# Eight of the 22 row tiles of a down projection taken by block products of half size

## The chip, the cores and the metric

One core of a Trainium2 chip runs the whole program. The metric is the device time of one execution in microseconds (us). The engines are named as in the profile: PE (matmuls), DVE (vector), ACT (scalar), POOL, and SP, which issues the weight transfers.

## What is computed

Five blocks of a transformer in a row, on 512 tokens of width 1024, all in fp32. Each block is a mixer (state space and banded attention in the first; stick-breaking, differential attention or a short convolution, and an attention over a memory, in the four of the second part) and then a gated feed-forward part, which is what the change touches:

```python
D_FF = -(-8 * D_MODEL // (3 * 256)) * 256        # 2816 = 22 tiles of 128
x = x + (jax.nn.silu(h2 @ w_gate[l]) * (h2 @ w_up[l])) @ w_down[l]

def _swiglu(x, w_in, w_out):
    gu = x @ w_in
    return (jax.nn.silu(gu[..., :D_FF_2]) * gu[..., D_FF_2:]) @ w_out
```

The five feed-forward parts have the same sizes: 1024 to 2 x 2816 and 2816 to 1024.

## The kernel before

Tensors lie with the feature on the partitions: `x` is 8 tiles of 128 features x 512 tokens. To keep fp32 accuracy every operand is split into a high part (rounded, made by ACT) and a low part (the rest, made by DVE as raw minus high), and every product is three matmuls: high x high, high x low, low x high. The code calls the parts `hh, hl`, `acth, actl`, `whi, wlo`, `wh, wl`.

Weights stream in *units*: 128 partitions x 2048 elements in one of two slots of `raw`. SP loads a unit when the low part of the unit before it is made (`lo_made`), ACT makes its high part when the unit that held the slot is used up (`unit_used`; `ahead`, `high`), DVE its low part (`low`), and PE waits for that (`unit_ready`). All engines run their own fixed program in order and meet at counting semaphores, so an instruction that waits holds up everything behind it on its engine.

A feed-forward part (`swiglu(s, u0, gc, r)` on each engine) has 34 units, u0 to u0+33. Units u0 and u0+1 are taken with plain matmuls. The next 20 units (10 turns of two, gate and up columns) go through `seven`: the 8 row tiles and the 2 column tiles of a unit are a 2 x 2 block matrix, and seven block products replace eight. A product is 4 row tiles x 3 matmuls of 256 tokens, 12 matmuls, and a unit has 84. PE's order in a unit is A11, S1, A22 *of the unit before*, S2, A12, S4, S3. For that DVE makes sums of weight blocks (`first_sums`, `sum_s2`, `sum_s4`), the low parts of all seven forms (`corner_low`, `sum_low`, `odd_low`, `sums_low`), a correction in PSUM of the unit before (`take_late`, counted by `late_made`, for which A22 waits), and the result of the unit before (`finish`): the gate goes to `gs`, and the product with the up half to `actr`, 22 tiles of unscaled activations. Turns 1 to 8 are a hardware loop; turns 0 and 9 are written out.

The down projection is two column halves of 512, each six units (five of 4 row tiles, one of 2), with 4 column tiles in 4 PSUM banks: 48 matmuls of 512 tokens in a full unit, 24 in the short one. `scale_tiles` multiplies `actr` by the row factor of the norm and a sign just before the high part of these tiles (`act_high`) and their low part (`act_low`, `tile_lows`) are made; `down_lows` puts scaling, `low` and `act_low` in a row for each unit. During the first unit of the down stage, PE does the last A22 product, and DVE finishes the last pair of tiles (20, 21).

## Time and profile before

| | |
|---|---|
| median of 3 runs | 3000.03 us (2999.93 to 3000.07) |
| the profiled execution | 3000.31 us, of which the span is 2998.6 us |
| granted clock of PE over the span | 0.999 |
| PE busy | 2982.5 us, 99% |
| DVE busy | 2086.0 us, 70% |
| ACT busy | 1384.7 us, 46% |
| DMA | 283.18 MB, mean 94 GB/s |

The span is what the profile shows of an execution; 1.7 us lie around it. Matmuls are pipelined, and the duration that a row shows for one (0.28 us at 256 tokens, 0.39 us at 512) is longer than the distance to the next one's start. A short wait of PE hides in that overlap and is not counted as idle, so the time of PE has to be read from starts, not from its busy time.

### The profile page before, as it was taken

The numbers are of one execution on the slowest core, as the hardware profiler recorded it, in microseconds if no ns is written. First come the engines' busy times: TensorE is split into PE (matmuls) and PEld (weight loads), VectorE is DVE, ScalarE is ACT, GpSimd is POOL, SyncE is SP. The second block draws the span as 40 slices with busy tenths as digits, with TensorE's granted clock in tenths as the row PEclk, the third lists the DMA queues.
The fourth block names the chain that finished last, engine by engine and source line by source line (L and its number), as shares of the span: only waits on it lengthen the run. The fifth ranks groups of instructions, "written<-read, shape, count | busy, mean of one in ns | idle before, by whom it ended". The sixth has DMA issues, their size and how long they took to land.

```text
span 2998.6 us, 46083 instructions
## 1 busy us (share of the span) xinstructions
PE 2982.5 (99%) x18093; PEld 2636.0 (88%) x18093; DVE 2086.0 (70%) x2497; ACT 1384.7 (46%) x1969; POOL 58.7 (2%) x148
## 2 busy tenths in 40 slices
PE   9999999999999999999999999999999999999998
PEld 8779998888889998878899988789998878899987
DVE  7978886466759884466598854658886457588862
ACT  3576553354445553334455533325554244365533
POOL 6100000000000000000000000000000000000000
PEclk9999999999999999999999999999999999999999
DMA  6122332342133233211333323223232222232322
GB/s 188 49 75 88 108 117 93 110 135 71 55 100 99 98 112 98 85 59 59 106 101 98 112 92 102 88 67 116 98 107 97 92 85 65 63 112 98 112 92 77
DMA packets 246445, 283.18 MB, mean 94 GB/s; under 512 B 11874, under 2 KB 208672, under 8 KB 246312
## 3 DMA queue, kind: packets, MB, share of 16 engines
q1 hardware_dynamic: 246200, 281.28, 29.2%
q8 instruction: 97, 1.59, 0.2%
q14 instruction: 36, 0.29, 0.0%
q10 hardware_dynamic: 112, 0.02, 0.0%
HBM read 279.16 MB, written 4.73 MB: 95 GB/s over the span
## 4 chain that ended last, share of the span: by engine, by line
PE 95%; DVE 3%; ACT 1%; issue 1%; DMA 0%; POOL 0%; ACTq 0%; POOLq 0%; SPq 0%; DVEq 0%
PE ps L2689 33%; PE ps L2318 17%; PE ps L2320 17%; PE ps L2319 17%; PE ps L2985 1%; PE ps L2986 1%; PE ps L2987 1%; PE ps L2892 1%; PE ps L2952 1%; PE ps L2931 1%; PE ps L2971 1%; PE ps L2972 1%; PE ps L2973 1%; PE ps L2821 1%; PE ps L2841 1%
## 5 line engine op out<-in xcount | busy, mean ns | idle before, releaser
L1390 DVE TENSOR_TENSOR wlo<-raw,whi 128x2048 fp32r<-128x2048 f32 (+2 forms) x169 | 350.8, 2076 | 415.6 <-ACT whi L787 415.3
L787 ACT ACTIVATE whi<-raw 128x2048 fp32r<-128x2048 f32 (+2 forms) x169 | 294.6, 1743 | 746.9 <-PE ps L2320 693.0
L2689 PE MATMUL ps<-th,wh 128*128 128x256 f32 x1600 | 453.7, 284 | 0.6 <-DVE wl L1475 0.5
L2689 PE MATMUL ps<-tl,wh 128*128 128x256 f32 x1600 | 452.7, 283 | 0.0
L2689 PE MATMUL ps<-th,wl 128*128 128x256 f32 x1600 | 452.7, 283 | 0.0
L2318 PE MATMUL ps<-hh,whi 128*128 128x512 f32 x896 | 357.3, 399 | 1.0 <-DVE uf L1857 1.0
L2320 PE MATMUL ps<-hh,wlo 128*128 128x512 f32 x896 | 349.7, 390 | 0.0
L2319 PE MATMUL ps<-hl,whi 128*128 128x512 f32 x896 | 349.3, 390 | 0.0
L2318 PE MATMUL ps<-acth,whi 128*128 128x512 f32 x880 | 342.7, 389 | 0.0
L2319 PE MATMUL ps<-actl,whi 128*128 128x512 f32 x880 | 342.5, 389 | 0.0
L2320 PE MATMUL ps<-acth,wlo 128*128 128x512 f32 x880 | 342.4, 389 | 0.0
L2689 PE MATMUL ps<-hh,wh 128*128 128x256 f32 x1200 | 340.0, 283 | 0.1
L2689 PE MATMUL ps<-hh,wl 128*128 128x256 f32 x1200 | 339.6, 283 | 0.0
L2689 PE MATMUL ps<-hl,wh 128*128 128x256 f32 x1200 | 339.6, 283 | 0.0
L2689 PEld LDWEIGHTS ps<-th,wh 128*128 128x128 f32 x1600 | 307.0, 192 | 2.3 <-DVE wl L1475 1.1
L2689 PEld LDWEIGHTS ps<-tl,wh 128*128 128x128 f32 x1600 | 307.0, 192 | 0.2
L2689 PEld LDWEIGHTS ps<-th,wl 128*128 128x128 f32 x1600 | 307.1, 192 | 0.0
L2689 PEld LDWEIGHTS ps<-hh,wh 128*128 128x128 f32 x1200 | 230.3, 192 | 0.8 <-DVE gs L1526 0.3
L2689 PEld LDWEIGHTS ps<-hl,wh 128*128 128x128 f32 x1200 | 230.4, 192 | 0.2
L2689 PEld LDWEIGHTS ps<-hh,wl 128*128 128x128 f32 x1200 | 230.3, 192 | 0.0
L2318 PEld LDWEIGHTS ps<-hh,whi 128*128 128x128 f32 x896 | 168.4, 188 | 38.8 <-issue 6.1
L2320 PEld LDWEIGHTS ps<-hh,wlo 128*128 128x128 f32 x896 | 168.2, 188 | 36.0
(472 smaller groups left out, 5706.5 us busy)
## 6 DMA issues: line engine op xcount, KB each, us to landing
raw<-in_w_ffn_in SPq DMA_DIRECT2D x88, 1024.0 KB, 5.1
raw<-in_w_in SPq DMA_DIRECT2D x59, 1024.0 KB, 5.3
raw<-in_w_ffn_out SPq DMA_DIRECT2D x40, 1024.0 KB, 5.0
raw<-in_w_o SPq DMA_DIRECT2D x32, 640.0 KB, 4.3
raw<-in_w_gate SPq DMA_DIRECT2D x11, 1024.0 KB, 5.3
raw<-in_w_up SPq DMA_DIRECT2D x11, 1024.0 KB, 5.4
raw<-in_w_down SPq DMA_DIRECT2D x10, 1024.0 KB, 5.0
raw<-in_w_mem_kv SPq DMA_DIRECT2D x8, 1024.0 KB, 5.4
```

What stands on the lines that cost most here:

```text
L787: a.activation(whi[:, slot, 0:n], raw[:, slot, 0:n], ACT.Copy).then_inc(hi_made, 1)
L1390: v.tensor_tensor(wlo[:, u % 2, 0:n], raw[:, u % 2, 0:n], whi[:, u % 2, 0:n].bitcast(F32), ALU.subtract).then_inc(lo_made, 1)
L2318: mm(dst, wh, xh, start=first, stop=False, skip_group_check=True)
L2319: mm(dst, wh, xl, start=False, stop=False, skip_group_check=True)
L2320: return mm(dst, wl, xh, start=False, stop=last, skip_group_check=True)
L2689: e = mm(bank(b, HALF), wgt[:, q, w], xx, start=start and k == 0 and m == 0, stop=k == KD // 2 - 1 and m == 2, skip_group_check=True)
L2821: e = mm(bank(b + r, MEM, MEM * i), mq[rows, f, t:t + P], km[rows, l, f, :], start=i == 0, stop=True, skip_group_check=True)
L2841: e = mm(ps[64 * r:64 * r + 64, o:o + 256], vm[:, l, j, MD * h:MD * h + MD], mt[:, j, 256 * r:256 * r + 256], start=j == 0, stop=j == 1, s ...
L2892: e = tr(ps[:, o:o + P], stick[:, ZQ[i] + P * j:ZQ[i] + P * j + P], ident[:, :])
L2931: e = mm(bank(6 + d, T - P * j, P * j), vp[hd % 2][:, j, P * d:P * d + P], dpt[:, ZK[j]:ZK[j] + wk(j)], start=j == 0, stop=j == 3, skip_gr ...
L2952: e = mm(ps[:, ZQ[i]:ZQ[i] + wq(i)], qp[hd % 2][:, c, P * i:P * i + P], kp[hd % 2][:, c, 0:wq(i)], start=i != 2, stop=True, skip_group_che ...
L2971: mm(dst, hs, whi[:, slot, w], start=k == 0, stop=False, skip_group_check=True)
```

## The change

In each of the five down projections the row tiles 8 to 15 are taken out of the two column halves. They are multiplied for all 1024 columns in four units of 8 row tiles x 256 columns, with seven half-size products each, like the units of the up loop. The order of units is now: column half 0 with row tiles 0 to 3, 4 to 7, 20 and 21, 16 to 19 (units u0+22 to u0+25); the four new units (u0+26 to u0+29); column half 1 with row tiles 0 to 3, 4 to 7, 16 to 19, 20 and 21 (u0+30 to u0+33). The number of units and of bytes is the same.

The result of a new unit is added to two tiles of `x` by DVE (`run_added`), column half 0 is added to `x` in `half_in`, and column half 1 as before. The new units need the activations in blocks: four sums of blocks of 4 tiles x 256 tokens (`run_t`), their high and low parts (`run_th`, `run_tl`), and the parts of the even and odd tiles (`even_hi`, `odd_hi`); `down_run` is DVE's program for this. Scaling leaves the down stage: turn i of the up loop, from 1 to 9, ends with the scaling of its pair of tiles; pair 10 is scaled at the start of `down_run`.

Two edits lie elsewhere: the first eviction of the first projection is cut in two, so that PE waits only for one tile, and the small operations `lambda_and_distance` of the differential attention come three slots earlier.

```diff
-                pair_loop(2, u0 + 22, 4, 512, lambda j: (wd, 4 * j, min(4, KF - 4 * j), 0, 512), per=6)
+                for d in range(12):
+                    u = u0 + 22 + d
+                    if 4 <= d < 8:
+                        load(u % 2, KD, 256, wd[:, 8:16, 256 * (d - 4):256 * (d - 4) + 256], u - 1)
+                    else:
+                        t, c0 = down_rows(d), 512 * (d >= 8)
+                        n = min(4, KF - t)
+                        load(u % 2, n, 512, wd[:, t:t + n, c0:c0 + 512], u - 1)
...
+                if j and not (isinstance(i, int) and i == 0):
+                    dve.wait_ge(acc_free, at_turn(i, 2, gc + 2))
+                    v.tensor_tensor(tiles_of_pair(i), tiles_of_pair(i), rs2[:, :, :], ALU.mult).then_inc(act_scaled, 1)
...
+            def run_added(s, u0, n):
+
+                dve.wait_ge(unit_used, u0 + 27 + n)
+                dve.wait_ge(late_made, LATES * s + 21 + n)
+                ab, bb, _ = RUN[n % 2]
+                first = v.tensor_tensor(x[:, 2 * n, :], x[:, 2 * n, :], bank(ab), ALU.add)
+                second = v.tensor_tensor(x[:, 2 * n + 1, :], x[:, 2 * n + 1, :], bank(bb), ALU.subtract)
+                if n < 2:
+                    first.then_inc(x_new, 1)
+                    second.then_inc(x_new, 1)
+                else:
+                    second.then_inc(acc_free, 1)
...
+            def down_run(s, u0, gc):
+
+                p, first = u0 % 2, u0 + 26
+                dve.wait_ge(acc_free, gc + 22)
+                v.tensor_tensor(tiles_of_pair(10), tiles_of_pair(10), rs2[:, :, :], ALU.mult).then_inc(act_scaled, 1)
+                dve.wait_ge(act_scaled, SCALED * s + 7)
+                dve.wait_ge(product_done, PRODUCTS * s + 120)
+                v.tensor_tensor(run_t[0][:, :, :], run_half(0, 0), run_half(0, 1), ALU.subtract).then_inc(sum_made, 1)
+                v.tensor_tensor(run_t[2][:, :, :], run_half(1, 1), run_half(0, 1), ALU.subtract).then_inc(sum_made, 1)
+                dve.wait_ge(sum_made, SUMS * s + 65)
+                v.scalar_tensor_tensor(out=run_t[1][:, :, :], in0=run_half(1, 1), scalar=-1.0, in1=run_t[0][:, :, :],
+                                       op0=ALU.mult, op1=ALU.subtract).then_inc(sum_made, 1)
+                dve.wait_ge(sum_made, SUMS * s + 67)
+                v.scalar_tensor_tensor(out=run_t[3][:, :, :], in0=run_t[1][:, :, :], scalar=-1.0, in1=run_half(1, 0),
+                                       op0=ALU.mult, op1=ALU.subtract).then_inc(sum_made, 1)
+                dve.wait_ge(ffn_hi, FFN_HIS * s + 20)
+                tile_lows(20, 2)
+                for k, t in enumerate((0, 2)):
+                    moved_low(s, t, 21 + k)
+                dve.wait_ge(ffn_hi, FFN_HIS * s + 23)
+                tile_lows(16, 4)
+                low(u0 + 24)
+                dve.wait_ge(sum_made, SUMS * s + 68)
+                for k, t in enumerate((1, 3)):
+                    moved_low(s, t, 24 + k)
+                dve.wait_ge(ffn_hi, FFN_HIS * s + 26)
+                v.tensor_tensor(actl[:, 8:16:2, 0:HALF], run_half(0, 0), even_hi[:, :, :].bitcast(F32), ALU.subtract).then_inc(ffn_lo, 1)
+                dve.wait_ge(ffn_hi, FFN_HIS * s + 27)
+                v.tensor_tensor(actl[:, 9:16:2, :], actr[:, 9:16:2, :], odd_hi[:, :, :].bitcast(F32), ALU.subtract).then_inc(ffn_lo, 1)
+                low(u0 + 25)
+                dve.wait_ge(loaded[p], 16 * (first // 2 + 1))
+                first_sums(p, True)
+                corner_low("A11", p, p, form_hi, FORM_HIS * s + 101, form_lo)
+                corner_low("A12", p, p, form_hi, FORM_HIS * s + 102, form_lo)
+                dve.wait_ge(sum_made, SUMS * s + 69)
+                sum_s2(p, p, True)
+                sum_low("S1", p, form_hi, FORM_HIS * s + 103, form_lo, True)
+                dve.wait_ge(sum_made, SUMS * s + 70)
+                sum_s4(p, p, True)
+                sum_low("S2", p, form_hi, FORM_HIS * s + 104, form_lo, True)
+                half_in(s, u0, gc, range(3))
+                sum_low("S4", p, form_hi, FORM_HIS * s + 105, form_lo, True)
+                corner_low("A22", p, p, form_hi, FORM_HIS * s + 106, lo_made)
+                for n in range(4):
+                    run_step(s, u0, gc, n)
+                dve.wait_ge(ffn_hi, FFN_HIS * s + 28)
+                low_half(u0 + 30, 0, ffn_lo)
+                run_late(s, 3)
+                dve.wait_ge(hi_made, plain_units(u0 + 30) + 1)
+                low_half(u0 + 30, 1, lo_made)
+                run_added(s, u0, 3)
+                low(u0 + 31)
...
                 tile_lows(0, 1)
-                scale_tiles(2, 2)
...
                 tile_lows(2, 2)
-                down_lows(s, u0, (1,))
+                low(u0 + 23)
+                dve.wait_ge(ffn_hi, FFN_HIS * s + 19)
+                tile_lows(4, 4)
                 dve.wait_ge(unit_used, u0 + 22)
...
                 finish(s, STREAMED, 1)
+                down_run(s, u0, gc)
...
-            down_lows(0, U_GU1, range(2, 8))
...
-                        v.tensor_tensor(phases, src.rearrange("p (a c s) -> p a c s", a=2, s=4), row, ALU.mult).then_inc(acc_free, 1)
+                        src = src.rearrange("p (a c s) -> p a c s", a=2, s=4)
+                        if u == 0:
+                            v.tensor_tensor(phases[:, 0:1], src[:, 0:1], row[:, 0:1], ALU.mult).then_inc(S("first_tile"), 1)
+                            phases, src, row = phases[:, 1:2], src[:, 1:2], row[:, 1:2]
+                        v.tensor_tensor(phases, src, row, ALU.mult).then_inc(acc_free, 1)
...
-                if s == DZ[0] - 2:
+                if s == DZ[0] - 5:
...
+            def run_unit(s, u0, gc, r, n):
+
+                p, (ab, bb, db) = u0 % 2, RUN[n % 2]
+                even = lambda k: (even_hi[:, k, :], actl[:, 8 + 2 * k, 0:HALF])
+                odd = lambda h: lambda k: (odd_hi[:, k, HALF * h:HALF * h + HALF], actl[:, 9 + 2 * k, HALF * h:HALF * h + HALF])
+                t_ = lambda m: lambda k: (run_th[m - 1][:, k, :], run_tl[m - 1][:, k, :])
+                form = lambda k: pe.wait_ge(form_lo, FORM_LOS * s + (80 + (1, 3, 2, 4, 5)[k] if n == 0 else 81 + 4 * n + (2, 3, 4, 4, 4)[k]))
+                snap = lambda k: pe.wait_ge(snap_taken, SNAPS * s + 60 + 3 * n + k)
+                form(0)
+                if n == 0:
+                    pe.wait_ge(acc_free, gc + 22)
+                    pe.wait_ge(ffn_lo, FFN_LOS * s + 19)
+                elif n == 1:
+                    pe.wait_ge(acc_free, gc + 23)
+                else:
+                    pe.wait_ge(x_new, KD * (r + 1) + 2 * n - 2)
+                product("A11", p, even, ab, start=True).then_inc(product_done, 1)
+                form(1)
+                product("S1", p, t_(1), db, start=True).then_inc(product_done, 1)
+                if n:
+                    run_corner(s, u0, n - 1)
+                form(3)
+                snap(1)
+                product("S2", p, t_(2), bb).then_inc(product_done, 1)
+                if n == 0:
+                    form(2)
+                else:
+                    pe.wait_ge(lo_made, u0 + 27 + n)
+                product("A12", p, odd(0), ab).then_inc(product_done, 1)
+                form(4)
+                snap(2)
+                product("S4", p, odd(1), db).then_inc(product_done, 1)
+                pe.wait_ge(form_lo, FORM_LOS * s + 86 + 4 * n)
+                snap(3)
+                product("S3", p, t_(3), bb).then_inc(product_done, 1)
...
+                    if d == 0:
+                        pe.wait_ge(acc_free, gc + 21)
+                    elif d < 4:
+                        unit_ready(u0 + 22 + d)
+                        pe.wait_ge(ffn_lo, FFN_LOS * s + (11, 12, 15)[d - 1])
+                    elif d == 8:
+                        pe.wait_ge(ffn_lo, FFN_LOS * s + 20)
+                        pe.wait_ge(acc_free, gc + 24)
+                    else:
+                        unit_ready(u0 + 22 + d)
...
+                for d in range(4):
+                    down(d)
+                for n in range(4):
+                    run_unit(s, u0, gc, r, n)
+                for d in range(8, 12):
+                    down(d)
```

The first place is the end of the loop of turns on DVE. Before, the last instructions of turn 8's second unit are the result to `gs` (L1526), the low parts of two corners (L1469) and of two sums (L1475); then the loop branches, a scaling of tiles 0 and 1 stands once behind the loop (L1642), and the correction for which A22 waits is L1516:

```order
L1469 TENSOR_TENSOR wl_57<-raw,wh_55 128x2x512
L1473 REGISTER_ALU
L1475 TENSOR_TENSOR wl_57<-stmp,wh_55 128x2x512
L1639 REGISTER_ALU
L1639 COMPARE_AND_BRANCH
L1642 TENSOR_TENSOR actr<-actr,rs_63 128x1024
L1516 TENSOR_TENSOR ps<-ps,us 128x2x256
```

In the changed kernel, where L1556, L1562 and L1603 are the same three operations:

```order
L1556 TENSOR_TENSOR wl_57<-raw,wh_55 128x2x512
L1560 REGISTER_ALU
L1562 TENSOR_TENSOR wl_57<-stmp,wh_55 128x2x512
L1653 REGISTER_ALU
L1654 TENSOR_TENSOR actr<-actr,rs_63 128x1024
L1826 REGISTER_ALU
L1826 COMPARE_AND_BRANCH
L1829 TENSOR_TENSOR actr<-actr,rs_63 128x1024
L1603 TENSOR_TENSOR ps<-ps,us 128x2x256
```

One scaling has come in ahead of the loop's branch, so it stands between L1562 and the L1603 of the next turn in every turn of the loop; behind the loop there are two in a row.

The second place is DVE in the first units of the down stage. Before, from the product of the last pair (L1524) on, with scalings (L1587), low parts of weight units (L1390) and of activations (L1573):

```order
L1524 TENSOR_TENSOR actr<-ps,gs 128x1024
L1587 TENSOR_TENSOR actr<-actr,rs_63 128x2048
L1390 TENSOR_TENSOR wlo<-raw,whi 128x2048
L1573 TENSOR_TENSOR actl<-actr,acth 128x2048
L1587 TENSOR_TENSOR actr<-actr,rs_63 128x2048
L1390 TENSOR_TENSOR wlo<-raw,whi 128x2048
```

In the changed kernel, up to the low part of weight unit u0+24 (L1476), for which PE's unit d = 2 waits. L1611 is the product of the last pair, L1723 its scaling, L1726 to L1732 are the block sums, L1775 and L1778 low parts of activations:

```order
L1611 TENSOR_TENSOR actr<-ps,gs 128x1024
L1723 TENSOR_TENSOR actr<-actr,rs_63 128x1024
L1726 TENSOR_TENSOR run_t_151<-actr 128x1024
L1727 TENSOR_TENSOR run_t_153<-actr 128x1024
L1729 SCALAR_TENSOR_TENSOR run_t_152<-actr,run_t_151 128x1024
L1732 SCALAR_TENSOR_TENSOR run_t_154<-run_t_152,actr 128x1024
L1778 TENSOR_TENSOR actl<-actr,acth 128x1024
L1775 TENSOR_TENSOR run_tl_159<-run_t_151,run_th_155 128x1024
L1775 TENSOR_TENSOR run_tl_161<-run_t_153,run_th_157 128x1024
L1778 TENSOR_TENSOR actl<-actr,acth 128x2048
L1476 TENSOR_TENSOR wlo<-raw,whi 128x1024
```

and from there to the low part of weight unit u0+25, which PE's unit d = 3 waits for:

```order
L1775 TENSOR_TENSOR run_tl_160<-run_t_152,run_th_156 128x1024
L1775 TENSOR_TENSOR run_tl_162<-run_t_154,run_th_158 128x1024
L1745 TENSOR_TENSOR actl<-actr,even_hi 128x4x256
L1747 TENSOR_TENSOR actl<-actr,odd_hi 128x4x512
L1476 TENSOR_TENSOR wlo<-raw,whi 128x2048
```

Between the product of the last pair and the next weight unit's low part there stood one scaling of 2048 elements; now there stand nine instructions there, and four between that low part and the following unit's, where two stood.

## Rows read from the trace of the kernel before

**Rows 1.** The page, part 1: engine, busy us (share of span) xinstructions.
```profile
PE 2982.5 (99%) x18093; PEld 2636.0 (88%) x18093; DVE 2086.0 (70%) x2497; ACT 1384.7 (46%) x1969; POOL 58.7 (2%) x148
```

**Rows 2.** Who the matmuls waited for, whole span: us, times, longest.
```profile
PE ps L2318 <- DVE uf L1857: 1.0, 1, 1.0
PE ps L2916 <- DVE lam L2111: 0.5, 1, 0.5
```

**Rows 3.** Timeline of ACT, up loop: start us, us, instruction, idle before.
```profile
383.06 0.37 ACT L880 ACTIVATE ps<-ps 128x256 f32<-128x256 f32 x1 [0.73 <-PE ps L2689]
...
390.34 1.06 ACT L859 ACTIVATE wh<-stmp 128x1024 fp32r<-128x1024 f32 x1 [0.31 <-PE ps L2689]
...
393.14 0.37 ACT L880 ACTIVATE ps<-ps 128x256 f32<-128x256 f32 x1 [0.81 <-PE ps L2689]
```

**Rows 4.** Timeline of ACT, down stage, two weight units in sequence.
```profile
474.92 1.92 ACT L787 ACTIVATE whi<-raw 128x2048 fp32r<-128x2048 f32 x1 [3.51 <-PE ps L2320]
...
485.80 1.92 ACT L787 ACTIVATE whi<-raw 128x2048 fp32r<-128x2048 f32 x1 [7.16 <-PE ps L2320]
```

**Rows 5.** Windows: one turn of the up loop, and most of the down stage.
```profile
320.84:341.00 20.16, 20.16 (x171) 20.16 (x170) 16.83 (x20) 11.06 (x17) 0.00 (x0) 1.00 0.33 104
474.64:530.00 55.36, 55.36 (x246) 45.83 (x245) 28.14 (x16) 20.77 (x16) 0.00 (x0) 1.00 0.29 94
```

**Rows 6.** Timeline of DVE, a steady boundary of two turns.
```profile
381.35 1.23 DVE L1475 TENSOR_TENSOR wl<-stmp,wh 128x1024 fp32r<-128x1024 f32 x1 [0.22 <-ACT wh L859]
382.49 0.69 DVE L1516 TENSOR_TENSOR ps<-ps,us 128x512 f32<-128x512 f32 x1
...
390.06 1.23 DVE L1469 TENSOR_TENSOR wl<-raw,wh 128x1024 fp32r<-128x1024 f32 x1 [1.48 <-ACT wh L856]
```

**Rows 7.** Timeline of PE: first matmuls of A22 and of S3.
```profile
384.30 0.28 PE L2689 MATMUL ps<-th,wh 128*128 128x256 f32 x1
...
390.06 0.28 PE L2689 MATMUL ps<-th,wh 128*128 128x256 f32 x1
```

**Rows 8.** Timeline of DVE, the boundary ahead of the last turn.
```profile
442.98 1.22 DVE L1642 TENSOR_TENSOR actr<-actr,rs 128x1024 f32<-128x1024 f32 x1
444.11 0.69 DVE L1516 TENSOR_TENSOR ps<-ps,us 128x512 f32<-128x512 f32 x1
```

**Rows 9.** Timeline of PE at that boundary, first and fifth swiglu.
```profile
444.66 0.28 PE L2689 MATMUL ps<-th,wl 128*128 128x256 f32 x1
444.95 0.35 PE L2689 MATMUL ps<-th,wh 128*128 128x256 f32 x1
445.14 0.28 PE L2689 MATMUL ps<-tl,wh 128*128 128x256 f32 x1
...
2845.92 0.28 PE L2689 MATMUL ps<-th,wl 128*128 128x256 f32 x1
2846.21 0.35 PE L2689 MATMUL ps<-th,wh 128*128 128x256 f32 x1
```

**Rows 10.** Source view of L1642: durations min/median/max ns, first and last start.
```profile
L1642 DVE TENSOR_TENSOR actr<-actr,rs x5: 1218/1218/1219, 443.0 to 2844.2; 128x1024 f32<-128x1024 f32 x5
```

**Rows 11.** Timeline of DVE, start of the down stage.
```profile
468.69 2.29 DVE L1390 TENSOR_TENSOR wlo<-raw,whi 128x2048 fp32r<-128x2048 f32 x1 [0.43 <-ACT whi L787]
470.90 2.28 DVE L1573 TENSOR_TENSOR actl<-actr,acth 128x2048 fp32r<-128x2048 f32 x1
473.10 1.22 DVE L1524 TENSOR_TENSOR actr<-ps,gs 128x1024 f32<-128x1024 f32 x1
474.24 2.28 DVE L1587 TENSOR_TENSOR actr<-actr,rs 128x2048 f32<-128x2048 f32 x1
```

**Rows 12.** Timeline of DVE, two scalar_tensor_tensor, the second needs the first.
```profile
248.78 1.22 DVE L1608 SCALAR_TENSOR_TENSOR traw<-hg,traw 128x1024 f32<-128x1024 f32 x1
250.03 1.22 DVE L1610 SCALAR_TENSOR_TENSOR traw<-traw,hg 128x1024 f32<-128x1024 f32 x1
```

**Rows 13.** Timeline of DVE: the eviction that L1857 is.
```profile
33.74 2.00 DVE L1857 TENSOR_TENSOR uf<-ps,rs 128x1024 f32<-128x1024 f32 x1
```

More of the change, by code:

```diff
@@ L369, in g_in @@
         def g_in(l):
-            return G_L0 + sum(evictions(m) + 22 for m in range(l))
+            return G_L0 + sum(evictions(m) + 25 for m in range(l))
         def g_gu(l):
@@ new lines, in sum_high, with moving_high, run_step @@
+            def sum_high(form, p, sem, run=False):
+                a.activation(wh8[:, place_of(form, p), :], temp_sum(run, form, p), ACT.Copy).then_inc(sem, 1)
+            def moving_high(s, t):
+                act.wait_ge(sum_made, SUMS * s + 65 + (0, 2, 1, 3)[t])
+                a.activation(run_th[t][:, :, :], run_t[t][:, :, :], ACT.Copy).then_inc(ffn_hi, 1)
+            def run_step(s, u0, n):
+                p, (ab, bb, db) = u0 % 2, RUN[n % 2]
+                slot = (u0 + n) % 2
+                done = lambda k: act.wait_ge(product_done, PRODUCTS * s + 120 + 6 * n + k)
+                summed = lambda k: act.wait_ge(sum_made, SUMS * s + 68 + 3 * n + k)
+                done(0)
+                summed(1)
+                sum_high("S3", p, form_hi, True)
+                done(1)
+                a.activation(bank(bb, HALF), bank(ab, HALF), ACT.Copy).then_inc(snap_taken, 1)
+                if n < 3:
+                    act.wait_ge(loaded[1 - slot], 16 * ((u0 + 27 + n) // 2 + 1))
+                    corner_high("A11", p, 1 - slot, form_hi)
+                done(2)
+                act.wait_ge(late_made, LATES * s + 20 + n)
+                a.activation(us[:, 1, 0:HALF], bank(db, HALF), ACT.Copy).then_inc(snap_taken, 1)
+                if n < 3:
+                    summed(4)
+                    sum_high("S1", p, form_hi, True)
+                done(3)
+                a.activation(us[:, 0, 0:HALF], bank(bb, HALF), ACT.Copy).then_inc(snap_taken, 1)
+                done(4)
+                if n == 3:
+                    high_half(u0 + 30, 0, ffn_hi)
+                    high_half(u0 + 30, 1, hi_made)
+                    return
+                act.wait_ge(unit_used, u0 + 26 + n)
+                odd_high(p, 1 - slot, 1 - n % 2)
+                done(5)
+                summed(6)
+                sums_high(p, True)
@@ new lines, in swiglu @@
+                moving_high(s, 0)
+                moving_high(s, 2)
+                act.wait_ge(unit_used, u0 + 22)
+                act_high(s, 16, 4, 9)
+                ahead(u0 + 22)
+                moving_high(s, 1)
+                moving_high(s, 3)
+                a.activation(even_hi[:, :, :], run_half(0, 0), ACT.Copy).then_inc(ffn_hi, 1)
+                a.activation(odd_hi[:, :, :], actr[:, 9:16:2, :], ACT.Copy).then_inc(ffn_hi, 1)
+                ahead(u0 + 23)
+                first = u0 + 26
@@ L975, in swiglu @@
+                sum_high("S4", p, form_hi, True)
+                corner_high("A22", p, p, form_hi)
+                for n in range(4):
+                    run_step(s, u0, n)
+                for d in range(7, 12):
+                    if d >= 8:
+                        ahead(u0 + 22, 0, 0, d)
+                    if d == 7:
+                        ahead(u0 + 29)
                         if between:
@@ L977, in swiglu @@
                         residual(r + 1, range(4))
+                    if d == 11:
+                        residual(r + 1, range(4, 7))
+                    if between and d in (9, 10):
+                        memory_high(range(4) if d == 9 else range(4, KD))
+                    if s == NL and d == 10:
+                        first_columns()
                 residual(r + 1, range(7, 8))
@@ L1395, in lows, with residual @@
                     low(u)
-            def residual(r, wait, src, mode, before={}, after={}, flush=(), amid={}):
+            def residual(r, wait, src, mode, before={}, after={}, flush=(), amid={}, given=0):
                 def finish(t):
```

350 lines of the change are left out of this document (195 added, 155 removed).

## The prediction

> **What bounds the kernel now.** I read the page's first part, then the list of waits of PE, then starts in the timeline. PE is busy 99% of the span and DVE 70% [rows 1]; the waits that the matmuls show are 1.0 us and 0.5 us at two single places, beside some smaller ones [rows 2]. So the time is the sum of PE's distances from start to start, and a change pays by fewer or shorter distances and costs by every wait that it puts on PE.
>
> Two distances price the change. In the up loop ACT copies the result of the first product of each unit (L880), once a unit: 383.06 and 393.14, so 84 matmuls of 256 tokens take 10.08 us, 0.120 us each [rows 3]. In the down stage ACT makes the high part of a weight unit when PE has left the unit before it: 474.92 and 485.80, so 48 matmuls of 512 tokens take 10.88 us, 0.2267 us each [rows 4]. ACT starts 0.28 us after PE is through: S3 starts on PE at 390.06, when S4 has ended, and ACT's L859, which waits for S4, at 390.34 [rows 3, 7]. So in the first feed-forward part PE leaves unit u0+22 at 474.92 - 0.28 = 474.64.
>
> **What is saved on PE.** 8 row tiles x 8 column tiles x 3 = 192 matmuls of 512 tokens are four full units, 43.52 us; the new ones are 4 x 10.08 = 40.32 us. Saved: 3.20 us for each of five parts, **16.0 us**. Transfers stay equal in number and bytes, and nothing in the down stage waits for them.
>
> The 256-token matmul here costs more than half of the 512-token one: half would be 0.1133 us, the row says 0.120 [rows 3, 4]. The Trainium skill ("TensorE: Matmul & The Clock Gate", Back-to-back issue gap) gives N / 2.4 + 2.5 ns for an isolated matmul at full clock, 109 ns and 216 ns. By its formula the saving would be 20 x (48 x 0.216 - 84 x 0.109) = 24 us, 8 us more. The row comes from the same form of product and decides.
>
> **What the scaling costs in the loop.** Per turn DVE is busy 16.83 of 20.16 us [rows 5], so 1.14 us more fits by the sum. But it is put where DVE is late. S4 of a unit ends on PE at 390.06 - 10.08 = 379.98; behind it come ACT's high part, DVE's low part of two sums (381.35), then the correction L1516, 382.49 to 383.18 [rows 6]. A22 waits for this correction and starts at 384.30 [rows 7]: 1.12 us of slack. The scaling is put between the two and takes 1.14 us. What that gives, the trace already shows, because L1642 is the same instruction in the same place, once in each part [rows 10]: it starts at 442.98, the correction moves to 444.11 to 444.80 [rows 8], PE starts A22 at 444.95 where 444.66 + 0.12 = 444.78 was due, and the next matmul follows after 0.19 instead of 0.12: 0.24 us lost, and the same 0.29 us distance stands in the fifth part [rows 9]. PE goes on 0.15 us after DVE's end.
>
> New scalings stand at the ends of turns 1 to 9. Those of turns 1 to 7 cost 0.24 us each, 1.68. That of turn 8 meets L1642, which stays behind the loop: two in a row, 1.14 us more in full. That of turn 9 is behind the last result, where DVE then waits for ACT's half unit anyway, and I cost it at nothing. Sum 2.82 us, times five **+14.1 us**. DVE does not fall behind further on, since it waits 1.48 us ahead of L1469 in the same turn [rows 6].
>
> **What DVE costs in the first down units.** DVE used to be idle nearly half of this stage: 28.14 of 55.36 us busy [rows 5]. The work for the new units comes in a burst. Lengths from start to start: 1.14 us for 1024 elements (473.10 to 474.24), 2.21 for 2048 (468.69 to 470.90) [rows 11], 1.25 for 1024 if the instruction needs the one before it (248.78 to 250.03) [rows 12]. The last pair's product starts at 473.10 as before, since nothing ahead of it on the path changes. From there, by the order shown: scaling of pair 10 at 474.35; four block sums at 475.49, 476.63, 477.77 and 479.02; low parts of tiles 20 and 21 at 480.16; of two sums at 481.30 and 482.44; of tiles 16 to 19 at 483.58; of weight unit u0+24 at 485.79, ended at 485.79 + 1.23 = 487.02. ACT, which takes 1.06 us for 1024 elements and 1.92 for 2048 [rows 3, 4], has the four copies after its copy of pair 10 and the unit's own high part done about 6 us after 475.5, ahead of DVE. PE needs the unit at 474.64 + 10.88 = 485.52 and gets it at 487.17: it waits **1.65 us**. It then has only the short unit, 24 matmuls, 5.44 us, to 492.61. DVE goes on: two low parts of sums at 486.93 and 488.07, even tiles at 489.21, odd tiles (2048) at 490.35, weight unit u0+25 at 492.56, ended at 494.85. PE gets it at 495.00 and waits **2.39 us** more. Sum 4.04 us, times five **+20.2 us**. I take the four other parts as equal, because the same instructions run there.
>
> The order of units makes this worse: the short unit, which gives DVE half the time, comes third, with the greatest backlog.
>
> **The new units themselves** I cost at nothing beyond their matmuls. Two additions of 512 elements take the place of the result of 1024, DVE's load per unit is that of a loop unit without scaling, and the first one has 3 us of room: DVE waits for PE to leave unit u0+25 for its last two low parts, S4 and A22, about 1.5 us after that, and S4 starts 4 x 1.44 = 5.8 us after. The going over to column half 1 is built like the one to column half 0, where PE's list of waits names nothing. Without that cover a unit would wait as the loop's boundary does, 0.24 us, 20 times: 5 us at most.
>
> **The two small edits.** The eviction that PE waits for 1.0 us [rows 2] takes 2.00 us [rows 13]; one tile of it takes half, so PE starts about 1 us sooner: -1.0, but this can be lost again in the attention that follows, where PE also waits for DVE. The lambda operations: -0.5 [rows 2], at least nothing. I take -1.5 together, with 0 as the other bound.
>
> **Sum.** 3000.31 of the profiled execution (span 2998.6 and 1.7 around it) - 16.0 + 14.1 + 20.2 - 1.5 = 3017.1; the median before is 0.3 below that execution, so 3016.8, rounded to **3017 us**, 0.57% slower.
>
> **Rivals.**
> *All hidden* (faster): PE's queue of loaded matmuls absorbs both waits, and only the saving is left, 3000.0 - 16.0 - 1.5 = 2982.5. For it: DVE has 30% idle over the span. Against it: L1642's wait is seen in every part, and the chain of DVE is a plain sum. Chance 0.08. It decides if DVE's burst were shorter by 4 us, for instance if the sums ran before the last pair's product.
> *Only one of the two waits is real* (no change): loop alone 2996.6, burst alone 3002.7. Chance 0.08.
> *The block products run at half the 512-token distance*, 0.1133 us: the saving is 20 x (10.88 - 9.52) = 27.2, and the time 3005.6. Nothing in the up loop speaks for it. Chance 0.02. The skill's formula above would be this side of the forecast, at 3009.
> *The new units wait too* (slower still): the chain of S4's and A22's forms, which starts only when u0+25 is used, or ACT, which has five copies there, makes PE wait 1 to 3 us per part: 3022 to 3032. Chance 0.12.
> *The clock falls* in the new waits: the granted clock is 1.00, so 2.4 GHz, in every window I read [rows 5], but none holds a wait of PE as long as 2.4 us. At 1.2 GHz a short unit of 5.44 us would cost 5.44 more, 27 us over five parts: 3044. Chance 0.02.
>
> **How the numbers follow.** The forecast, both waits real, has 0.68, with a range of its own of 3009 to 3022: the loop term between 0.17 and 0.30 us per turn (+-2.5), the burst between 3.2 and 4.6 us per part (+-4), the small edits 0 to 1.5. The whole range goes down over the half-distance case and up into the fourth rival: 3002 to 3026, which takes in the burst alone. A difference of 0.2%, 6 us, is what a measurement of this kernel tells from no change. Faster 0.08; within 0.2% (2994 to 3006) 0.10; slower 0.82.
>
> **What would show it.** In the changed trace: PE starts at A22 0.29 us after the matmul before it in turns 2 to 8 of each part, and some 1.4 us in turn 9; L1603 as the releaser. Waits of PE for L1476 of about 1.7 and 2.4 us at the third and fourth down unit, DVE without a gap from L1611 to the second of these. Units of 10.08 us and no waits between u0+26 and u0+29. The prediction is wrong if DVE shows gaps in that burst, if PE waits in the new units, or if no A22 is late in the loop.

## The result, and the profile after

The changed kernel takes 3019.11 us in the median of 5 runs (3018.17 to 3023.17), where the kernel before takes 3000.03 us in 5 runs beside it (2999.11 to 3000.45). The ratio is 1.0067, with a 95% interval of 1.0056 to 1.0079: slower by 19 us. The profiled execution took 3019.11 us, with a span of 3017.4 us. The forecast of 3017 us held.

Part 1 of the page answers to [rows 1], and the list of PE's waits over the span (us, times, longest) to [rows 2]:

```profile
PE 2979.5 (99%) x18813; PEld 2660.8 (88%) x18813; DVE 2254.2 (75%) x2773; ACT 1459.1 (48%) x2144; POOL 58.0 (2%) x148
```

```profile
PE ps L2509 <- DVE wlo L1476: 18.1, 13, 2.1
PE ps L2884 <- DVE ps L1603: 5.7, 5, 1.1
```

PE's busy time has gone down by 3 us and the span has gone up by 19, so the time lies in waits. DVE grew from 70% to 75% of the span, far from full. Both waits of [rows 2] are gone (L1857 and the lambda), and two new ones head the list. The wait for L1603 comes once in each of the five parts. That for L1476 comes twice in each (17.0 us together); the three other times are short ones, 0.35 us each, at the start of a layer (experiment 7).

**The loop.** PE at the correction's boundary, in a steady turn of part 1, in turn 9, and in a steady turn of part 2 (starts; the answer to [rows 9]):

```profile
303.01 0.28 PE L2884 MATMUL ps<-th,wl 128*128 128x256 f32 x1
303.30 0.36 PE L2884 MATMUL ps<-th,wh 128*128 128x256 f32 x1
303.49 0.28 PE L2884 MATMUL ps<-tl,wh 128*128 128x256 f32 x1
...
445.81 0.28 PE L2884 MATMUL ps<-th,wl 128*128 128x256 f32 x1
447.23 0.36 PE L2884 MATMUL ps<-th,wh 128*128 128x256 f32 x1 [1.15 <-DVE ps L1603]
...
953.48 0.28 PE L2884 MATMUL ps<-th,wl 128*128 128x256 f32 x1
953.67 0.39 PE L2884 MATMUL ps<-th,wh 128*128 128x256 f32 x1
953.90 0.28 PE L2884 MATMUL ps<-tl,wh 128*128 128x256 f32 x1
```

Two distances of 0.12 us are 0.24. At 303.01 they take 0.48: 0.24 us are lost, with no idle time shown, as forecast; for that reason the profile names no releaser in these turns. In part 2, and in the same way in parts 3 to 5, they take 0.42, so 0.18 is lost. In turn 9 the first distance alone is 1.42: 1.30 us lost, and 0.07 more at the next. DVE shows why: the scaling stands between the low part that A22's turn needs and the correction (compare [rows 6], where L1516 came 1.14 us behind L1475; here L1603 comes 2.28 behind L1562).

```profile
320.58 1.23 DVE L1562 TENSOR_TENSOR wl<-stmp,wh 128x1024 fp32r<-128x1024 f32 x1 [0.22 <-ACT wh L885]
321.72 1.22 DVE L1654 TENSOR_TENSOR actr<-actr,rs 128x1024 f32 x1
322.86 0.69 DVE L1603 TENSOR_TENSOR ps<-ps,us 128x512 f32<-128x512 f32 x1
```

**The burst.** DVE in the first down units, from the product of the last pair on (the answer to [rows 11]), and PE where it waits:

```profile
475.37 1.22 DVE L1611 TENSOR_TENSOR actr<-ps,gs 128x1024 f32<-128x1024 f32 x1
476.62 1.23 DVE L1723 TENSOR_TENSOR actr<-actr,rs 128x1024 f32<-128x1024 f32 x1
477.76 1.22 DVE L1726 TENSOR_TENSOR run_t<-actr 128x1024 f32<-128x1024 f32 x1
478.90 1.22 DVE L1727 TENSOR_TENSOR run_t<-actr 128x1024 f32<-128x1024 f32 x1
...
481.29 1.22 DVE L1732 SCALAR_TENSOR_TENSOR run_t<-run_t,actr 128x1024 f32<-128x1024 f32 x1
...
488.04 1.22 DVE L1476 TENSOR_TENSOR wlo<-raw,whi 128x1024 fp32r<-128x1024 f32 x1
...
494.78 2.28 DVE L1476 TENSOR_TENSOR wlo<-raw,whi 128x2048 fp32r<-128x2048 f32 x1
```

```profile
487.59 0.39 PE L2511 MATMUL ps<-acth,wlo 128*128 128x512 f32 x1
489.31 0.50 PE L2509 MATMUL ps<-acth,whi 128*128 128x512 f32 x1 [1.33 <-DVE wlo L1476]
489.65 0.39 PE L2510 MATMUL ps<-actl,whi 128*128 128x512 f32 x1
...
494.66 0.39 PE L2511 MATMUL ps<-acth,wlo 128*128 128x512 f32 x1
497.12 0.50 PE L2509 MATMUL ps<-acth,whi 128*128 128x512 f32 x1 [2.07 <-DVE wlo L1476]
```

DVE has no gap from 475.37 to the second weight unit. The matmul at 489.31 was due at 487.59 + 0.23 = 487.82: 1.49 us of wait. The one at 497.12 was due at 494.89: 2.23 us. The next matmul follows 0.34 us behind instead of 0.227, another 0.1 us each time. The idle figures in brackets (1.33, 2.07) are smaller than the waits, since the row's duration of 0.39 covers part of them.

The Trainium skill ("Perfetto Trace Analysis", Optimizing Scalar/DVE Operations) puts some 60 ns of data access on a DVE operation in SBUF and says that a profiled latency is longer than that, because the end of one operation overlaps the next; from that and the Trainium skill's 0.96 GHz for DVE ("VectorE: DVE Perf Modes", Specifications) an estimate for an operation of 1024 elements is 1.13 us. The rows agree: they last 1.22 us and follow each other after 1.14.

**The new units.** ACT's copy of the first product, once a unit, in units u0+27 and u0+28 (the answer to [rows 3]):

```profile
518.40 0.37 ACT L905 ACTIVATE ps<-ps 128x256 f32<-128x256 f32 x1 [0.81 <-PE ps L2884]
...
528.49 0.37 ACT L905 ACTIVATE ps<-ps 128x256 f32<-128x256 f32 x1 [0.81 <-PE ps L2884]
```

10.09 us, and the list shows no wait of PE in these units. Read from starts, the 336 matmuls of the four units follow each other after 0.120 us in the mean in every part, and none after more than 0.14 but one: there the first twelve matmuls of column half 1 stand ahead of the last A22 product.

**What the forecast did not have.** In part 2 the matmuls behind the second wait run at twice their distance (PE, starts), and the windows around it (length; PE, PEld, DVE, ACT and POOL busy; PE's granted clock; DMA share; GB/s) show the granted clock:

```profile
1147.92 0.45 PE L2509 MATMUL ps<-acth,whi 128*128 128x512 f32 x1
1148.17 0.63 PE L2510 MATMUL ps<-actl,whi 128*128 128x512 f32 x1
1148.60 0.63 PE L2511 MATMUL ps<-acth,wlo 128*128 128x512 f32 x1
...
1151.16 0.57 PE L2511 MATMUL ps<-acth,wlo 128*128 128x512 f32 x1
1151.56 0.39 PE L2509 MATMUL ps<-acth,whi 128*128 128x512 f32 x1
```

```profile
1140.00:1147.50 7.50, 5.43 (x25) 4.16 (x24) 7.50 (x6) 1.57 (x3) 0.00 (x0) 1.00 0.42 140
1147.50:1151.50 4.00, 4.00 (x12) 3.16 (x11) 4.00 (x7) 1.26 (x2) 0.00 (x0) 0.58 0.81 254
1151.50:1155.00 3.50, 3.50 (x17) 2.85 (x16) 1.47 (x3) 0.00 (x0) 0.00 (x0) 1.00 0.04 13
```

The distance is 0.43 us there instead of 0.227, for 3.4 us: the clock was at 1.2 GHz, and 8 matmuls cost 8 x 0.2 = 1.6 us more. The four other parts show nothing of the kind in this execution.

### The profile page after: what moved, and what is told of

It reads as the page before. It is cut to its first block, busy times and chain, and to the rows that moved or that the text cites. A ratio compares the mean times of both kernels' runs of the same rounds, so it can differ in the third digit from the quotient of the medians.

```text
span 3017.4 us, 48033 instructions
## 1 busy us (share of the span) xinstructions
PE 2979.5 (99%) x18813; PEld 2660.8 (88%) x18813; DVE 2254.2 (75%) x2773; ACT 1459.1 (48%) x2144; POOL 58.0 (2%) x148
## 4 chain that ended last, share of the span: by engine, by line
PE 86%; DVE 9%; issue 2%; ACT 2%; POOL 1%; DMA 0%; ACTq 0%; DVEq 0%; POOLq 0%; SPq 0%
PE ps L2884 39%; PE ps L2509 12%; PE ps L2511 12%; PE ps L2510 12%; DVE wlo L1476 2%; PE ps L3237 1%; PE ps L3238 1%; PE ps L3239 1%; DVE actl L1778 1%; PE ps L3144 1%; DVE run_tl L1775 1%; ACT whi L818 1%; PE ps L3204 1%; PE ps L3183 1%; PE ps L3223 1%
## 5 line engine op out<-in xcount | busy, mean ns | idle before, releaser
L818 ACT ACTIVATE whi<-raw 128x2048 fp32r<-128x2048 f32 (+2 forms) x144 | 246.5, 1712 | 501.4 <-PE ps L2511 424.0
L1476 DVE TENSOR_TENSOR wlo<-raw,whi 128x2048 fp32r<-128x2048 f32 (+2 forms) x144 | 293.5, 2038 | 220.4 <-ACT whi L818 220.1
L2509 PE MATMUL ps<-acth,whi 128*128 128x512 f32 x560 | 220.1, 393 | 17.0 <-DVE wlo L1476 17.0
L2510 PE MATMUL ps<-actl,whi 128*128 128x512 f32 x560 | 218.9, 391 | 0.0
L2511 PE MATMUL ps<-acth,wlo 128*128 128x512 f32 x560 | 218.6, 390 | 0.0
L1556 DVE TENSOR_TENSOR wl<-raw,wh 128x1024 fp32r<-128x1024 f32 x110 | 134.6, 1223 | 89.0 <-ACT wh L882 88.3
```

The lines of the kernel that those rows point to most:

```text
L818: a.activation(whi[:, slot, 0:n], raw[:, slot, 0:n], ACT.Copy).then_inc(hi_made, 1)
L1476: v.tensor_tensor(wlo[:, u % 2, 0:n], raw[:, u % 2, 0:n], whi[:, u % 2, 0:n].bitcast(F32), ALU.subtract).then_inc(lo_made, 1)
L1556: v.tensor_tensor(blocks_of_two(wl8[:, q, :]), odd_corners(slot, p), blocks_of_two(wh8[:, q, :]).bitcast(F32), ALU.subtract).then_inc(lo_m ...
L2509: mm(dst, wh, xh, start=first, stop=False, skip_group_check=True)
L2510: mm(dst, wh, xl, start=False, stop=False, skip_group_check=True)
L2511: return mm(dst, wl, xh, start=False, stop=last, skip_group_check=True)
```

## Experiments

Two theories stood at the start. The first is the prediction's: nothing but DVE's order costs the time, in two places that add up, 12 to 14 us in the loop and 19 to 20 in the burst. The rival: the new units cost something beyond their rows (more instructions, more DMA beside them, a slower matmul), and the waits are only where it shows; then a kernel without the two waits would still not reach some 2985 us. The times stand beside runs of the kernel before on the same chip: 2999.83 us in the median for the first four kernels and 2999.83 for the other four. The changed kernel itself was not run again beside them.

**1. The scaling earlier in the turn.** It stands right behind the result of the unit before, where DVE has 1.48 us of idle time ([rows 6]), and not between L1562 and L1603:

```diff
+                if j and not (isinstance(i, int) and i == 0):
+                    dve.wait_ge(acc_free, at_turn(i, 2, gc + 2))
+                    v.tensor_tensor(tiles_of_pair(i), tiles_of_pair(i), rs2[:, :, :], ALU.mult).then_inc(act_scaled, 1)
...
-                if j and not (isinstance(i, int) and i == 0):
-                    dve.wait_ge(acc_free, at_turn(i, 2, gc + 2))
-                    v.tensor_tensor(tiles_of_pair(i), tiles_of_pair(i), rs2[:, :, :], ALU.mult).then_inc(act_scaled, 1)
```

Expected: 

> The changed kernel with one edit: the scaling of a turn's pair of tiles stands right behind the result to gs of the turn's second unit, where DVE waits 1.4 us for ACT anyway, and no longer behind the low parts of the two sums. Same instructions, same count. Theory (the place of the scaling delays the correction for which A22 waits): the eight waits per part go but for the one of 0.18 to 0.24 us that L1829 alone makes, 12.5 us over five parts, so about 3006. Rival (the loop is slower because DVE has more instructions and register work in it): stays at 3018 to 3019.

Measured: 3009.34 us (3007.69 to 3012.44, 8 runs), 1.0031 times before (1.0020 to 1.0042). DVE at a boundary of two turns:

```profile
377.11 1.21 DVE L1649 TENSOR_TENSOR actr<-actr,rs 128x1024 f32 x1
378.60 1.23 DVE L1556 TENSOR_TENSOR wl<-raw,wh 128x1024 fp32r<-128x1024 f32 x1 [0.28 <-ACT wh L882]
380.04 1.22 DVE L1562 TENSOR_TENSOR wl<-stmp,wh 128x1024 fp32r<-128x1024 f32 x1 [0.21 <-ACT wh L885]
381.18 0.69 DVE L1603 TENSOR_TENSOR ps<-ps,us 128x512 f32<-128x512 f32 x1
```

The same scalings fill the idle time ahead of L1556 (0.28 is left of it), L1603 follows L1562 at 1.14 us again, and no wait for L1603 is left in the list. So the loop's cost is the place of the scaling, not its work. The gain is 9.8 us where some 12 were due, and the time is 3 us above the one expected: the trace of this kernel has half-clock stretches behind the second wait in two parts (1744.38 to 1747.79 and 2901.53 to 2904.93), where that of the changed kernel had one. One stretch more, some 1.7 us, covers most of what is missing.

**2. The burst in another order.** The parts of tiles 20, 21 and of weight unit u0+24 come first, then the block sums, and the low parts of the sums stand behind the weight unit that PE needs next. ACT's copies are ordered alike, and PE's unit d = 3 waits for the low parts of tiles 16 to 19 by their new number.

```diff
+                dve.wait_ge(ffn_hi, FFN_HIS * s + 20)
+                tile_lows(20, 2)
+                low(u0 + 24)
...
-                for k, t in enumerate((0, 2)):
-                    moved_low(s, t, 21 + k)
-                dve.wait_ge(ffn_hi, FFN_HIS * s + 23)
+                dve.wait_ge(ffn_hi, FFN_HIS * s + 21)
                 tile_lows(16, 4)
-                low(u0 + 24)
+                moved_low(s, 0, 22)
+                low(u0 + 25)
+                moved_low(s, 2, 23)
```

Expected: 

> The changed kernel with the order of DVE's and ACT's work in the first four down units changed, and nothing else: the low part of weight unit u0+24 comes right behind the low part of tiles 20 and 21, ahead of the block sums, and that of u0+25 behind the first of the sums' low parts, ahead of the other three and of the even and odd tiles. Theory (PE waits because these two low parts stand at the end of a burst that nobody needs before unit u0+26): the waits of 1.49 and 2.23 us per part go, 18.6 us, and the falls of the clock behind them, so about 2999. Rival (DVE's load in this stage is too high in any order, so the wait moves to unit u0+26): 3012 or more, with a wait of PE at the first block product.

Measured: 2997.04 us (2996.67 to 2997.95, 10 runs), 0.9990 (0.9980 to 1.0000). DVE, the two weight units:

```profile
479.48 1.22 DVE L1476 TENSOR_TENSOR wlo<-raw,whi 128x1024 fp32r<-128x1024 f32 x1
...
489.39 2.29 DVE L1476 TENSOR_TENSOR wlo<-raw,whi 128x2048 fp32r<-128x2048 f32 x1 [0.69 <-ACT whi L818]
```

```profile
PE ps L2884 <- DVE ps L1603: 5.7, 5, 1.1
...
PE ps L2509 <- DVE wlo L1476: 1.0, 3, 0.4
```

Counted from the product of the last pair (L1611, here at 474.73), the low part of the first unit starts 7.9 us earlier than in the changed kernel and that of the second 4.8; what is left for L1476 in the list are three short waits elsewhere. The same instructions ran. This takes 22.1 us off the changed kernel: more than the 19.7 of the two waits, and the half-clock stretch is gone with them. The edit moves ACT's copies as well; that DVE's order held PE, and not ACT's, is read from the changed kernel, where DVE has no gap in the burst, and from experiment 8.

**3. Both orders.** The two edits together.

Expected: 

> Both edits of e1_scale_early and e2_burst_order. Theory: the terms add, since they lie in different stages: 3018 - 12.5 - 18.6 = 2987, faster than before by the 16 us of matmuls less what is left. Rival (the saving of 16 us on PE is not real, the block products of the new units cost as much as the plain ones): about 3003.

Measured: 2984.75 us (2984.58 to 2984.93, 4 runs), 0.9948 (0.9931 to 0.9964). The two waits are gone from the list, and the kernel is 15 us faster than before. The rival falls: the new units cost what their rows say, to within some tenths of a us for each part. With no new wait in the feed-forward parts, this trace also gives the saving itself. From the first matmul of `seven` to the last of the down stage, in part 1 (kernel before, then this one):

```profile
261.45 0.28 PE L2689 MATMUL ps<-hh,wh 128*128 128x256 f32 x1
...
585.03 0.39 PE L2320 MATMUL ps<-acth,wlo 128*128 128x512 f32 x1
```

```profile
260.19 0.28 PE L2884 MATMUL ps<-hh,wh 128*128 128x256 f32 x1
...
580.75 0.39 PE L2511 MATMUL ps<-acth,wlo 128*128 128x512 f32 x1
```

323.58 us have become 320.56. The same two rows in each part and kernel give this table of what each kernel needs more than the one before, in us:

| part | changed kernel | 1, scaling early | 2, burst order | 3, both |
|---|---|---|---|---|
| 1 | +3.81 | +0.94 | -0.29 | -3.02 |
| 2 | +4.84 | +0.83 | -0.86 | -3.05 |
| 3 | +3.16 | +2.46 | -0.76 | -3.17 |
| 4 | +3.57 | +1.18 | -0.50 | -2.82 |
| 5 | +3.16 | +2.44 | -0.85 | -3.27 |
| sum | +18.54 | +7.85 | -3.26 | -15.33 |

The saving is 15.3 us. Split at the first matmul of the down stage (462.30 and 461.17 in part 1), the down stage alone takes 3.08 to 3.16 us less in each part, 15.7 together where 16.0 were forecast, and the up stages take 0.4 more. The loop costs 15.33 - 3.26 = 12.1 us. The burst costs 3.9 us in a part without half clock (parts 1, 2 and 4: 0.94 + 3.02, 0.83 + 3.05, 1.18 + 2.82), so 5 x 3.95 = 19.7.

**4. The scaling alone.** The kernel before, with only the scaling moved from the down stage into the loop (pair 10 is scaled behind its product, and ACT's waits count the scalings anew):

```diff
-                    if d < 6:
-                        scale_tiles(4 * d, 2 if d == 5 else 4)
...
-                scale_tiles(2, 2)
...
+                if j and not (isinstance(i, int) and i == 0):
+                    dve.wait_ge(acc_free, at_turn(i, 2, gc + 2))
+                    v.tensor_tensor(tiles_of_pair(i), tiles_of_pair(i), rs2[:, :, :], ALU.mult).then_inc(act_scaled, 1)
```

Expected: 

> The kernel before with one part of the change alone: the scaling moved into the loop of turns, in the place that the change gives it, and pair 10 scaled behind its product; the down projection as before. Theory: slower than before by the loop's waits alone, 12.5 us, so 3012.5; the scalings that leave the down stage give nothing back, since DVE waited there. Rival (the wait in the loop comes from something else in the change): 3000.

Measured: 3011.86 us (3011.80 to 3012.30, 5 runs), 1.0038 (1.0024 to 1.0052). PE at a steady boundary:

```profile
385.05 0.28 PE L2691 MATMUL ps<-th,wl 128*128 128x256 f32 x1
385.34 0.36 PE L2691 MATMUL ps<-th,wh 128*128 128x256 f32 x1
385.54 0.28 PE L2691 MATMUL ps<-tl,wh 128*128 128x256 f32 x1
```

The same 0.25 us as in the changed kernel, in a program without block products in the down stage: the loop's term, 12.0 us, is a cost of this one part of the change.

**5. The short unit last.** Tiles 20 and 21 change places with 16 to 19 in column half 0, so that the short unit is the fourth. The third is then a full one, which leaves PE busy for 10.9 us while DVE goes on (the number of low parts that PE waits for follows):

```diff
-        return 2 * 512 if u - U_DN1 in (2, 11) else UNIT
+        return 2 * 512 if u - U_DN1 in (3, 11) else UNIT
...
-            return (0, 4, 20, 16)[d] if d < 4 else (0, 4, 16, 20)[d - 8]
+            return (0, 4, 16, 20)[d] if d < 4 else (0, 4, 16, 20)[d - 8]
```

Expected: 

> The changed kernel with the order of two down units exchanged: row tiles 16 to 19 (48 matmuls) third and tiles 20 and 21 (24 matmuls) fourth; DVE's order is unchanged, so its weight unit u0+24 now has 2048 elements and u0+25 has 1024. Theory (the short unit in third place gives DVE half the time): the first wait grows by the longer low part, from 1.49 to about 2.55 us, the second is gone, since PE is busy 10.9 us behind it; 1.2 us less per part, so 3012, six below the changed kernel without falls of the clock. Rival (only the sum of DVE's burst counts, not where PE's work lies): 3018.

Measured: 3016.28 us (3014.28 to 3017.16, 4 runs), 1.0055 (1.0038 to 1.0071), 4 us more than expected. PE and a window behind the wait:

```profile
489.63 0.77 PE L2509 MATMUL ps<-acth,whi 128*128 128x512 f32 x1 [2.40 <-DVE wlo L1476]
490.20 0.63 PE L2510 MATMUL ps<-actl,whi 128*128 128x512 f32 x1
```

```profile
490.00:494.00 4.00, 4.00 (x12) 3.12 (x12) 4.00 (x4) 0.00 (x0) 0.00 (x0) 0.61 0.79 265
```

The order of units works as said: one wait of 2.55 us a part in place of 1.49 + 2.23, the second is gone. But behind it the clock is at half in three of five parts (1, 4 and 5: 490.20 to 493.16, 2302.15 to 2305.53, 2903.87 to 2906.39). Measured as in the table above, these three parts need 3.94, 4.50 and 3.33 us more than before, and the two others 1.86 and 1.88. Together that is 6.2 us, of which 0.4 is the costlier loop of part 1; the rest covers the 4 us that the expectation lacked.

**6. The small edits alone.** The kernel before, with the cut eviction and the earlier lambda operations (PE's waits for the two tiles of the eviction follow).

```diff
+                        if u == 0:
+                            v.tensor_tensor(phases[:, 0:1], src[:, 0:1], row[:, 0:1], ALU.mult).then_inc(S("first_tile"), 1)
+                            phases, src, row = phases[:, 1:2], src[:, 1:2], row[:, 1:2]
...
-                if s == DZ[0] - 2:
+                if s == DZ[0] - 5:
```

Expected: 

> The kernel before with the two small edits alone (the first eviction cut in two, the lambda operations three slots earlier). Theory: both waits that they take away, 1.0 and 0.5 to 0.7 us, stay away to the end, as the distance of the two traces says (-0.7 at the first block product, -0.7 behind the second part): 2998.4. Rival (they are lost again in the attention): 2999.9.

Measured: 2998.16 us (2997.60 to 2998.86, 10 runs), 0.9995 (0.9985 to 1.0004). The medians are 1.7 us apart, and both waits of [rows 2] are gone, but the interval of the ratio takes in 1: the size rests on the traces, where the changed kernel's first block product starts 0.70 us earlier than before (260.75 against 261.45; 260.44 in this experiment). Behind part 2 this kernel gains 1.3 us more: 0.7 where PE waited for the lambda and 0.6 at a matmul 3 us later. The changed kernel gains the same 1.3 there, but only 0.7 of it is left at the start of part 3, since 0.6 had been lost just before (experiment 7). So the two edits are worth 0.7 + 1.3 = 2.0 us by the traces and 1.7 by the medians.

**7. Both orders, and ACT's order in the last down unit.** Experiment 3 still had a wait that the kernel before hasn't, at the start of the layers behind parts 2, 3 and 4 (the expectation counted two of the three). Here are the ones behind parts 2 and 3:

```profile
1234.67 0.50 PE L2509 MATMUL ps<-hh,whi 128*128 128x512 f32 x1 [0.35 <-DVE wlo L1476]
...
1832.60 0.50 PE L2509 MATMUL ps<-hh,whi 128*128 128x512 f32 x1 [0.34 <-DVE wlo L1476]
```

From starts, PE loses 0.59 us at each of the three. In the changed kernel ACT makes the next layer's weights (`ahead`) ahead of the last three tiles of `residual`; before, it was the other way round in all parts but the first. The edit puts that back:

```diff
+                    if d == 11 and s:
+                        residual(r + 1, range(4, 7))
...
-                    if d == 11:
+                    if d == 11 and not s:
                         residual(r + 1, range(4, 7))
```

Expected: 

> e3_both with one more edit: in the last down unit of parts 2 to 5 ACT takes the high parts and squares of tiles 4 to 6 of x ahead of the high part of the weight unit after next, as in the kernel before. Theory: the wait of 0.59 us of PE at the start of the two layers that follow parts 3 and 4 goes, 1.2 us, so 2983.6. Rival (it comes from somewhere else): 2984.8.

Measured: 2983.09 us (2982.43 to 2983.99, 4 runs), 0.9945 (0.9929 to 0.9962). L1476 is gone from the list of PE's waits. It is 1.7 us below experiment 3 where 1.2 were expected for two waits; three of 0.59 us are 1.8. It is the fastest kernel here, 17 us below the one before. That step lies near what runs can tell; the vanished waits are what shows it.

**8. A longer wait.** The changed kernel with one more DVE operation of 1024 elements, which nothing needs, ahead of weight unit u0+25:

```diff
+                v.tensor_tensor(gs[:, :, :], rs2[:, :, :], rs2[:, :, :], ALU.mult)
                 low(u0 + 25)
```

Expected: 

> The changed kernel with one DVE instruction of 1024 elements more in each part, right ahead of the low part of weight unit u0+25; its result is not used. Theory: the second wait grows from 2.23 to 3.37 us, 5.7 us over five parts, 3024 if the clock stays; and the clock falls behind this wait in more of the five parts than in the changed kernel's profile (one of five), each fall costing 1.7 us as there, so 3024 to 3032, the most likely 3030. Rival (the fall at 1147 us had nothing to do with the wait): 3024, and the runs spread as before.

Measured: 3030.15 us (3029.22 to 3030.96, 4 runs), 1.0102 (1.0085 to 1.0118). PE in part 2, and a window:

```profile
1149.98 0.79 PE L2510 MATMUL ps<-acth,whi 128*128 128x512 f32 x1 [3.21 <-DVE wlo L1476]
1150.57 0.63 PE L2511 MATMUL ps<-actl,whi 128*128 128x512 f32 x1
```

```profile
1150.00:1156.00 6.00, 6.00 (x15) 4.70 (x16) 5.17 (x8) 1.27 (x2) 0.00 (x0) 0.52 0.54 178
```

One more operation of 1.14 us lengthens the wait in part 2 by 1.14 (2.07 to 3.21 idle): the burst is a plain sum on DVE. That gives 5.7 us over five parts. The time went up by 11: four parts of five now have a half-clock stretch (one before), in part 2 a longer one than before (1150.57 to 1155.69).

## Why the prediction was right

| term | predicted | measured | by |
|---|---|---|---|
| fewer and shorter matmuls | -16.0 | -15.3 | distances in experiment 3 |
| scaling in the loop | +14.1 | +12.1 | experiment 2 less 3; experiment 4: 12.0 |
| burst in the down units | +20.2 | +19.7 | experiment 1 less 3, parts at full clock |
| small edits | -1.5 | -2.0 | starts in the traces; experiment 6: -1.7 |
| ACT's order behind parts 2, 3 and 4 | none | +1.8 | three waits of 0.59 us; experiment 7: 1.7 |
| half clock behind the second wait | none | +1.7 | part 2 of the changed kernel |
| sum | +17 | +18 | span of the trace: +18.8 |

**Saved on PE.** Right: a new unit takes 10.09 us where 10.08 was forecast, and the rows of the up loop priced it. The half-distance rival falls with it. So does the formula that the prediction cited from the Trainium skill ("TensorE: Matmul & The Clock Gate"): it would have made the saving 24 us, and the five parts show 15.3. The saving is 0.7 below the forecast, 0.3 of it in the down stage; where the rest goes in the up stages was not followed up.

**The loop.** The mechanism was right: A22 late in turns 2 to 8, a full operation more in turn 9. L1603 is named as the releaser in turn 9 alone; in turns 2 to 8 it follows from the starts and from experiment 1. The size was high, since the 0.24 us of [rows 9] holds in part 1 and is 0.18 in the others (0.42 less 0.24 at 953.48), where I took all parts as equal, and so the 0.29 us distance that was to show it comes in part 1 alone. The rows narrow the difference down: L1603 ends at 322.86 + 0.69 = 323.55 in part 1 and PE's second matmul of A22 starts at 323.70, 0.15 us behind it; in part 2 it ends at 953.62 and PE goes on at 953.67, after 0.05. That the fifth part's boundary showed the same 0.29 as the first one's was no evidence for the boundaries of the loop itself.

**The burst.** Right: 1.49 and 2.23 us where 1.65 and 2.39 were forecast, DVE without a gap. From L1611 to the end of the first weight unit it took 13.9 us, as summed. Most of the 0.16 is that PE starts 0.05 us after DVE's end (489.26 and 489.31) and not 0.15; the slower matmul behind each wait, 0.1 us, which the sum did not have, gives most of it back.

**New units at nothing.** Right, as the list of waits and the starts show. **The small edits** gave 2.0 us by the traces where 1.5 was forecast, since the earlier lambda took away a second loss of 0.6 us behind the one in [rows 2].

**Rivals.** That PE hides both waits, or one of them, is refuted by experiments 1 to 3: each wait taken away gave its own price. The medians give 9.8 and 22.1 us for one edit each and 34.4 for both; in part 1, which is at full clock in all four kernels, the table adds up (2.87 and 4.10 for one edit each, 6.83 for both). Of the 2.5 us that the medians leave over, the half-clock stretch that experiment 1's trace has more than the changed kernel's covers some 1.7. It was the order, not DVE's load: experiment 3 runs the same DVE instructions and is 34 us faster than the changed kernel. **The clock's fall** had 0.02 as a fall in every part, at 27 us. It came in one part of five at 1.7 us, so as a case it didn't happen, but the wait of 2.4 us should have carried a term for a fall in some parts, 0 to 8 us. Such falls may also be behind the spread of the runs: the highest of the changed kernel, 4.1 us above the median, has a granted clock of 0.997 over its span where the four others have 0.998, and the highest of experiment 1 has 0.996 where the others have 0.997 or 0.998. But the run 2.7 us above the median has 0.998 as well, so three digits suggest this and don't show it.

**What was missed.** The order of ACT in the last down unit, 1.8 us: the diff has it, and I read the order of instructions only where DVE had new work.

Open is why the first part loses 0.24 us a turn and the others 0.18. No kernel was made for it.

## What to carry to other kernels

Judge an operation that is added to an engine by the slack between it and the next instruction that another engine waits for, not by the engine's busy share: the scalings, nine in a part's loop, cost 12 us over the five parts in one place of the turn and next to nothing about 4 us earlier, while DVE works 75% of the span. When a stage needs a burst of preparation, put what the matmuls need next ahead of what they need two units later, and let a long unit, not a short one, cover it. Such a change is worth building in a second order before it is judged: here the first order lost 19 us and the best one gained 17.

## What the hardware showed that was not expected

The granted clock fell to half behind single waits of PE of 2.2 to 3.4 us, between stretches in which PE had worked without a wait. With the second wait at 2.2 us (2.07 idle) it happened in 1 of 5 parts of the changed kernel and 2 of 5 of experiment 1; with 2.55 us (2.40 idle) in 3 of 5; with 3.3 to 3.4 us (3.17 to 3.21 idle) in 4 of 5; behind the waits of 1.5 us or less, in the same parts, never. Counted by the rows at the doubled distance a stretch lasted 2.1 to 5.1 us, and the one in the changed kernel, 3.4 us, cost some 1.6 us. So here a wait of more than 2 us could cost more than its length, and not in the same way in each pass through the same code.
